# Branch and output GEMMs of two token mixers: fp32 matmuls replaced by three fp32r passes, with the low weight parts on GpSimd

## The chip, the core and the metric

The kernel runs on one core of a Trainium2 chip. The metric is device time in microseconds (us) of one execution; the kernel before took 2956.33 us (median of three runs, 2955.53 to 2958.14). The engines are named as in the profile: PE is TensorE's matmul, PEld its weight load, DVE is VectorE, ACT is ScalarE, POOL is GpSimd, and SP is SyncE, which here issues all the DMAs.

## The reference, cut to what matters

The program is a stack of two blocks of a conditioned transformer and then two blocks of a second model. The change touches only the end of `token_mixer`, which runs once in each of the first two blocks (`l` is 0 or 1; S is 256 tokens, the model width is 1024):

```python
def token_mixer(h, w_in, pool_w, pool_scale, rel_bias, lb, norm_g, w_branch, w_out):
    proj = h @ w_in
    ...
    y_a = pool_mixer(a, pool_w, pool_scale)            # 256 wide
    y_b = sparse_attention(q, k, v, qi, ki, wi, ...)   # 256 wide
    y_c = hgrn2(hq, hf, hi, hg, lb, norm_g)            # 512 wide
    g = jax.nn.sigmoid(gates.reshape(B, S, 3, D_MODEL))
    merged = (g[:, :, 0] * (y_a @ w_branch[:256])
              + g[:, :, 1] * (y_b @ w_branch[256:512])
              + g[:, :, 2] * (y_c @ w_branch[512:]))
    return merged @ w_out
```

All inputs and outputs are fp32.

## The kernel before, in words

Every engine has a hand-written program of its own, and semaphores order them. Activations lie feature by feature: 128 features on the partitions, 256 tokens along the free dimension. A weight matrix is read in panels of 1024 rows by 256 columns (1 MB), which SP loads into four slots in turn; slot n is loaded again when the panel four places earlier has been used (`load_static`). Four PSUM banks (`acc`) are used in turn as well.

Large GEMMs are already *split*: ACT copies each half panel (1024 x 128) into an fp32r tile, the high part (`high`), another engine subtracts it from the half panel, which gives the low part in place (`low`), and PE runs three fp32r matmuls: high weights by high data, high by low, low by high. In the first two blocks the low parts are made by DVE; in the second model's "even" and "up0" GEMMs by POOL. The gate, branch and output GEMMs of the mixers are plain: one fp32 matmul for each 128 x 128 weight tile and 256 tokens.

The end of the mixer, in the order of the program:

- `pool(l)`, `attention(l)` and `hgrn(l)` give `ymix`, eight groups of 128 features: groups 0 and 1 from the pool mixer, 2 and 3 from attention, 4 to 7 from hgrn. Between them stands `stage_end`, a barrier of PE, ACT and DVE. PE works on panels of the gate GEMM (`gate`) in between.
- `hgrn(l)` is a tree of eight levels (`lv` 0 to 7). At each level ACT takes two exponentials, DVE adds twice into running sums (`suff`, `pref`) and multiplies twice into `treeX` (all four of these DVE operations read two tiles in SBUF), and PE multiplies tiles of `treeX`. After level 7 PE forms the output (line 974), does gate panel 11, and spreads the norm (line 851).
- after a barrier comes the branch GEMM: 4 panels, each of 16 matmuls in three groups (`r` 0, 1, 2 for y_a, y_b, y_c), each group into its own bank. For each group DVE multiplies the bank by the gate (line 86, from PSUM) and, for `r` 1 and 2, adds the product to `merged` (line 86, two SBUF tiles).
- after another barrier comes the output GEMM `mixout` (4 panels of 16 matmuls, in `features`, line 674); DVE adds each panel to the residual (line 91), PE sums it for the layer norm.
- in between DVE carries the conditioning sums (`cond_weigh`, line 2115): scalar_tensor_tensor operations on 1024 elements that read a loaded panel and a row, both in SBUF. Layer 0 has one such step of two operations after each of the first three branch panels and one in front of each mixout residual; layer 1 has none at the branch, and a step of four operations at each mixout panel. SP loads their panels too, in one queue with the weights (`load_cond`), and waits there for the step before last (`cond_done`).

Of the kernel before, what the change touches and what calls it, by code (L numbers as in the profile page):

```python
# [20 lines left out]
P = 128  # L21
# [120 lines left out]
def plan():  # L142

    order = []
    for l in range(DEPTH):
        order += [Gemm(f"in{l}0", 22, split=True, kept=True), Gemm(f"out{l}0", 8, wide=True, panels_per_acc=2, split=True, kept=True),
                  Gemm(f"mix{l}", 15, split=True), Gemm(f"gate{l}", 12), Gemm(f"branch{l}", 4, 3), Gemm(f"mixout{l}", 4),
# [69 lines left out]
def program(nc, io):  # L217
    G, order, finished, _ = plan()
    w8, w11, wc = io["w8"], io["w11"], io["wc"]
    with ExitStack() as ctx:  # L220
# [120 lines left out]
        merged, mtmp = region(TMP, KD, T), region(TMP + 2048, 2, T)  # L341

# [154 lines left out]
        def split_parts(g, u, j):  # L497

            if g.name in kept_hi:
                hi = kept_hi[g.name][:, :, j * P:j * P + P]  # L500
            else:
                hi = (down_hi if g.wide else up_hi)[(2 * u + j) % 4]
            return hi, half_panel(g, u, j, slots_r)
# [5 lines left out]
        def wait_used(eng, g, it, u, j):  # L509
# [3 lines left out]
            elif g.ppa == 1:  # L513
                a = g.a0 + u
                eng.wait_ge(ready[a % BANKS], it + (a // BANKS + 1))
# [14 lines left out]
        def _(sp):  # L530
# [56 lines left out]
            for g in order:  # L587
# [35 lines left out]
                if g.name == "mix0":  # L623
                    sp.wait_ge(S("pair_ready"), 1)
                    for v, kept in enumerate((crow_d, crow2_d)):
                        sp.dma_start(kept.ap().rearrange("a (k t) -> a k t", k=4), pair_rows[v][0:1, :, :]).then_inc(S("row_stored"), 16)
                if g.name == "in00":
# [3 lines left out]
                    sp.wait_ge(S("bias_rows"), 1)  # L631
# [10 lines left out]
        def _(pe):  # L642
# [133 lines left out]
            def mix_tokens(g, u):  # L776
# [4 lines left out]
                for tb in range(2):  # L781
# [9 lines left out]
                    if tb == 1:  # L791
                        mm.then_inc(ready[b], 1)

# [213 lines left out]
            def ml_columns():  # L1007
# [6 lines left out]
                mm.then_inc(S("ml_cols"), 1)  # L1014
# [185 lines left out]
            def ssd_rates():  # L1200
                pe.wait_ge(S("dt_rows"), 1)
# [118 lines left out]
            for l in range(DEPTH):  # L1320
                for f in range(2):
                    if f == 1:
# [27 lines left out]
                        stage_end(pe, count)  # L1350
                        g = G[f"branch{l}"]
                        for u in range(4):
                            w = panel_in(g, 0, u)
                            for r, ks in enumerate((range(0, 2), range(2, 4), range(4, 8))):
                                b = acc_open(g, 0, u, r)
                                for j in range(2):
                                    for k in ks:
                                        mm = pe.matmul(acc[b][:, j * T:j * T + T], w[:, k * PANEL + j * P:k * PANEL + j * P + P],  # L1358
                                                       ymix[:, k, :], start=(k == ks[0]), stop=(k == ks[-1]))
                                mm.then_inc(ready[b], 1)  # L1360
                        stage_end(pe, count)
                        g = G[f"mixout{l}"]
                        for u in range(4):
                            features(g, 0, u, lambda k: merged[:, k, :], T)
# [6 lines left out]
                    def up_panel(it, u, name=f"in{l}{f}"):  # L1371
                        split_up(G[name], it, u, 2 * l + f)
                        if name == "in00" and isinstance(it, int) and (it, u) == (0, 3):
                            pe.wait_ge(S("loaded"), 64)
                            pe.matmul(mix[0:4, 0, 0:384], relb[:, :], const("onehot")[0:32, :], start=True, stop=True).then_inc(S("bias_mm"), 1)
# [1773 lines left out]
```

## Time and profile before

| what | value |
|---|---|
| median of the timed runs | 2956.33 us |
| span of the profiled execution | 2961.5 us (the profile holds this one execution, from its first to its last instruction) |
| PE busy | 2736.3 us (92%) |
| DVE busy | 1931.9 us (65%) |
| ACT busy | 1091.3 us (37%) |
| POOL busy | 183.3 us (6%) |
| mean granted PE clock | 0.977 |

An fp32 matmul of 128 x 256 leaves two records in the trace, an fp32r matmul one. A row of the timeline has its start and its duration in us (of a merged run of instructions, from the first start to the last end), then the engine, the line, the operation, output and inputs, the shape, the count, and in brackets the idle time before it and what ended it. `L476` in brackets is the barrier.

### The profile page before, as it was taken

The numbers are of one execution on the slowest core, as the hardware profiler recorded it, in microseconds if no ns is written. First come the engines' busy times: TensorE is split into PE (matmuls) and PEld (weight loads), VectorE is DVE, ScalarE is ACT, GpSimd is POOL, SyncE is SP. The second block draws the span as 40 slices with busy tenths as digits, with TensorE's granted clock in tenths as the row PEclk, the third lists the DMA queues.
The fourth block names the chain that finished last, engine by engine and source line by source line (L and its number), as shares of the span: only waits on it lengthen the run. The fifth ranks groups of instructions, "written<-read, shape, count | busy, mean of one in ns | idle before, by whom it ended". The sixth has DMA issues, their size and how long they took to land.

```text
span 2961.5 us, 48706 instructions
## 1 busy us (share of the span) xinstructions
PE 2736.3 (92%) x18394; PEld 2322.9 (78%) x18394; DVE 1931.9 (65%) x3303; ACT 1091.3 (37%) x1389; POOL 183.3 (6%) x85
## 2 busy tenths in 40 slices
PE   3999998999999988999988968999999899989998
PEld 3998977899999887799967854687744767668887
DVE  6776655677778666466746473577786676664781
ACT  2434432443543423154463542433300644442211
POOL 0000000000000000000012300244200000000000
PEclk9999999999999999999999989999999999999999
DMA  8775734677676553345512201122377221113442
GB/s 305 260 282 216 274 107 163 220 265 282 230 261 242 196 185 113 132 167 211 201 68 70 87 15 37 64 97 87 112 262 286 83 75 58 58 57 127 145 167 73
DMA packets 106383, 469.14 MB, mean 158 GB/s; under 512 B 7052, under 2 KB 57304, under 8 KB 58328
## 3 DMA queue, kind: packets, MB, share of 16 engines
q1 hardware_dynamic: 106200, 466.67, 43.7%
q8 instruction: 119, 1.95, 0.3%
q14 instruction: 64, 0.52, 0.1%
HBM read 465.58 MB, written 1.06 MB: 158 GB/s over the span
## 4 chain that ended last, share of the span: by engine, by line
PE 35%; DVE 10%; DVEq 7%; ACT 3%; issue 3%; ACTq 1%; DMA 1%; SPq 0%
PE accs L828 6%; DVEq L2830 4%; PE accs L689 4%; PE accs L674 4%; PE accs L690 4%; PE accs L691 4%; DVE arena L2807 3%; PE accs L1225 2%; PE accs L1227 2%; PE accs L1226 2%; DVE arena L2115 1%; PE accs L1358 1%; ACT arena L76 1%; PE mix L1282 1%; DVE arena L86 1%
## 5 line engine op out<-in xcount | busy, mean ns | idle before, releaser
L689 PE MATMUL accs<-normed_r,arena_r 128*128 128x256 f32 (+2 forms) x1864 | 585.0, 314 | 17.7 <-DVEq L2160 6.3
L691 PE MATMUL accs<-normed_r,panel_r 128*128 128x256 f32 (+2 forms) x1872 | 584.7, 312 | 0.0
L690 PE MATMUL accs<-arena_r 128*128 128x256 f32 x2069 | 584.5, 283 | 0.0
L86 DVE TENSOR_TENSOR panel_r<-panel,arena_r 128x1024 fp32r<-128x1024 f32 (+1 forms) x295 | 387.1, 1312 | 165.6 <-ACTq L1478 120.3
L1477 ACT ACTIVATE arena_r<-panel 128x1024 fp32r<-128x1024 f32 (+1 forms) x292 | 330.4, 1132 | 331.6 <-DMA panel<-w 145.3
L689 PEld LDWEIGHTS accs<-normed_r,arena_r 128*128 128x128 f32 (+1 forms) x1864 | 350.2, 188 | 55.4 <-issue 13.5
L690 PEld LDWEIGHTS accs<-arena_r 128*128 128x128 f32 x2069 | 389.5, 188 | 1.1 <-issue 0.2
L691 PEld LDWEIGHTS accs<-normed_r,panel_r 128*128 128x128 f32 (+1 forms) x1872 | 350.2, 187 | 23.8 <-issue 0.8
L674 PE MATMUL accs<-normed,panel 128*128 128x256 f32 x1536 | 344.5, 384 | 6.7 <-ACTq L476 3.0
L2807 DVE SCALAR_TENSOR_TENSOR arena<-accs,vectors,arena 128x189 f32<-128x189 f32 (+2 forms) x704 | 279.3, 428 | 95.4 <-issue 66.2
L674 PEld LDWEIGHTS accs<-normed,panel 128*128 128x128 f32 x1536 | 291.8, 192 | 54.1 <-issue 4.6
L1437 POOL TENSOR_TENSOR panel_r<-panel,arena_r 128x1024 fp32r<-128x1024 f32 x70 | 169.1, 2416 | 1953.7 <-ACTq L1485 1952.4
L828 PE MATMUL accs<-arena,panel 128*128 128x256 f32 (+1 forms) x832 | 256.3, 469 | 1.4 <-DVEq L2715 0.8
L828 PEld LDWEIGHTS accs<-arena,panel 128*128 128x128 f32 x832 | 157.9, 190 | 98.2 <-issue 85.8
L76 ACT ACTIVATE arena<-accs 128x512 f32<-128x512 f32 (+2 forms) x128 | 75.3, 589 | 372.4 <-PE accs L691 234.8
L689 PE MATMUL accs<-arena_r 128*128 128x256 f32 x704 | 200.1, 284 | 6.3 <-DVEq L2160 6.2
L691 PE MATMUL accs<-arena_r,panel_r 128*128 128x256 f32 x704 | 198.3, 282 | 0.0
L91 DVE SCALAR_TENSOR_TENSOR residual<-accs,mods,residual 128x256 f32<-128x256 f32 x96 | 46.4, 483 | 179.5 <-PE accs L828 86.8
L76 ACT ACTIVATE arena<-arena 128x512 f32<-128x512 f32 (+7 forms) x108 | 97.5, 903 | 162.6 <-DVEq L2753 58.6
L76 ACT ACTIVATE arena<-residual 128x512 f32<-128x512 f32 (+1 forms) x56 | 31.9, 569 | 328.6 <-DVEq L2860 279.1
L1484 ACT ACTIVATE arena_r<-panel 128x1024 fp32r<-128x1024 f32 x72 | 76.3, 1060 | 203.9 <-PE accs L691 188.1
L689 PEld LDWEIGHTS accs<-arena_r 128*128 128x128 f32 x704 | 133.2, 189 | 9.1 <-issue 5.3
(412 smaller groups left out, 4701.3 us busy)
## 6 DMA issues: line engine op xcount, KB each, us to landing
panel<-w SPq DMA_DIRECT2D x250, 1024.0 KB, 5.0
panel<-w SPq DMA_DIRECT2D x48, 1408.0 KB, 8.0
cond_panel<-wc SPq DMA_DIRECT2D x57, 1024.0 KB, 6.3
normed<-wc SPq DMA_DIRECT2D x43, 1024.0 KB, 6.8
arena<-wc SPq DMA_DIRECT2D x19, 1024.0 KB, 5.0
residual<-xs SPq DMA_DIRECT2D x2, 1024.0 KB, 9.7
residual<-wc SPq DMA_DIRECT2D x1, 1024.0 KB, 13.2
residual<-crows SPq DMA_DIRECT2D x2, 512.0 KB, 8.8
```

Source lines behind the costliest of these rows:

```text
L76: i = self.eng.activation(*a, **k)
L86: i = self.eng.tensor_tensor(*a, **k)
L674: mm = pe.matmul(acc[b][:, o:o + ntok], w[:, k * PANEL + j * P:k * PANEL + j * P + P], rhs(k), start=(k == 0), stop=(k == KD - 1))
L689: pe.matmul(out, hi[:, k, 0:m], src_hi(k), start=clear and k == 0, stop=False, skip_group_check=True)
L690: pe.matmul(out, hi[:, k, 0:m], src_lo(k), start=False, stop=False, skip_group_check=True)
L691: mm = pe.matmul(out, lo[:, k, 0:m], src_hi(k), start=False, stop=last and k == n - 1, skip_group_check=True)
L828: mm = pe.matmul(acc[a % BANKS][:, o:o + ntok], w[:, k * PANEL + j * P:k * PANEL + j * P + P], src(part * kper + k), start=first, stop=(pa ...
L1437: pool.tensor_tensor(lo, half_panel(g, u, j), hi, ALU.subtract)
L1477: act.eng.activation(split_parts(g, u, j)[0], half_panel(g, u, j), ACT.Copy)
L1484: act.eng.activation(split_parts(g, u, j)[0], half_panel(g, u, j), ACT.Copy)
L2807: dve.eng.scalar_tensor_tensor(out=out, in0=src, scalar=scale, in1=out, op0=ALU.mult, op1=ALU.add)
L2830: dve.drain()
```

## The change

Both GEMMs become split GEMMs of three fp32r passes. ACT makes all high parts: of `ymix`, of `merged`, and of the 16 half panels of each layer (in a ring of four tiles, `merge_ring`). POOL makes the low parts of `ymix` groups 0 to 3 and of all the half panels; DVE makes those of `ymix` groups 4 to 7 and of `merged`. The two barriers around the branch GEMM go; semaphores (`ymix_low`, `ymix_tail`, `merged_high`, `merged_low`, `low_made`) order the engines instead. The product that gives `ymix` groups 4 to 7 is done in two halves. To have enough semaphores, a number of one-shot ones elsewhere are merged into counting ones (`setup_act`, `decay_act`, `rates_dve` and so on); the order of work there is as before.

The core of the diff:

```diff
-... Gemm(f"branch{l}", 4, 3), Gemm(f"mixout{l}", 4),
+... Gemm(f"branch{l}", 4, 3, split=True), Gemm(f"mixout{l}", 4, split=True),
+        merged_hi, merged_lo = region(TMP + 2560, KD, T, of=arena_r), region(4096, KD, T, of=arena_r)
+        ymix_hi, ymix_lo = mix_hi, mix_lo
+        merge_ring = [region(off, KD, P, of=arena_r) for off in (0, 1024, 2048, TMP + 5888)]
...
 (PE)
+            def branch(l):
+                g = G[f"branch{l}"]
+                for u in range(4):
+                    for r, ks in enumerate((range(0, 2), range(2, 4), range(4, 8))):
+                        b = acc_open(g, 0, u, r)
+                        for j in range(2):
+                            if r == 0:
+                                pe.wait_ge(S("low_made"), split_count(g, 0, u, j))
+                            hi, lo = split_parts(g, u, j)
...
+                                pe.matmul(out, hi[:, k, :], ymix_hi[:, k, :], ...)
+                                pe.matmul(out, hi[:, k, :], ymix_lo[:, k, :], ...)
+                                mm = pe.matmul(out, lo[:, k, :], ymix_hi[:, k, :], ...)
+                            if r == 2 and j == 0:
+                                mm.then_inc(first_used, 1)
+                        mm.then_inc(ready[b], 1)
+            def mixed_out(l, u):
...
+                        if u == 0 and j == 0 and k % 2 == 0:
+                            pe.wait_ge(S("merged_low"), 4 * l + k // 2 + 1)
...
                         hgrn(l)
-                        stage_end(pe, count)
...
+                        branch(l)
-                        stage_end(pe, count)
 (POOL)
+            for l in range(DEPTH):
+                for n in range(2):
+                    pool.wait_ge(S("ymix_high"), 2 * l + n + 1)
+                    c = slice(2 * n, 2 * n + 2)
+                    pool.tensor_tensor(ymix_lo[:, c, :], ymix[:, c, :], ymix_hi[:, c, :], ALU.subtract)
+                    pool.drain().then_inc(S("ymix_low"), 1)
+                for name in ("branch", "mixout"):
+                    for u in range(4):
+                        low(G[f"{name}{l}"], 0, u)
 (ACT, at the end of pool, at the end of attention, in the levels of hgrn)
+                act.activation(ymix_hi[:, 0:2, :], ymix[:, 0:2, :], ACT.Copy).then_inc(S("ymix_high"), 1)
+                act.activation(ymix_hi[:, 2:4, :], ymix[:, 2:4, :], ACT.Copy).then_inc(S("ymix_high"), 1)
+                    if lv in (6, 7):
+                        high(G[f"branch{l}"], 0, lv - 6)
+            def branch(l):
+                for h in range(2):
+                    act.wait_ge(S("ymix_made"), 2 * l + h + 1)
+                    ... ymix_hi of two groups, then_inc(S("ymix_tail_high"), 1)
+                high(g, 0, 2)
+                high(g, 0, 3)
+                for u in range(4):
+                    act.wait_ge(S("merged"), 4 * l + u + 1)
+                    ... merged_hi of two groups, then_inc(S("merged_high"), 1)
+                    if u in (1, 2):
+                        for j in range(2):
+                            wait_used(act, g, 0, u + 1, j)
+                            high(out, 0, u - 1, (j,))
+                for u in range(2, 4):
+                    high(out, 0, u)
 (DVE)
+            def merged_low(l, u):
+                c = slice(2 * u, 2 * u + 2)
+                dve.wait_ge(S("merged_high"), 4 * l + u + 1)
+                dve.tensor_tensor(merged_lo[:, c, :], merged[:, c, :], merged_hi[:, c, :], ALU.subtract).then_inc(S("merged_low"), 1)
...
                     if u < CARRY.get(g.name, (0, 0))[1]:
                         cond_weigh(g.name, u, u % 2)
+                    if u >= 1:
+                        merged_low(l, u - 1)
+                merged_low(l, 3)
```

Where instructions move, three places matter.

POOL, from the start of the program (all its instructions up to the first loop). Before, after the constants, it has only the low parts of the second model's panels:

```order
L3141 MEMSET const-uint8-127 128x1
L1430 UNCONDITIONAL_BRANCH
L1437 ISA
L1437 TENSOR_TENSOR panel_r<-panel,arena_r 128x8x128 x26
L486 UNCONDITIONAL_BRANCH
```

And now; `decay_sums_r` is where `ymix_hi` and `ymix_lo` lie, and of the 16 low parts of a layer 8 belong to the branch GEMM and 8 to mixout:

```order
L1464 UNCONDITIONAL_BRANCH
L1478 ISA
L1478 TENSOR_TENSOR decay_sums_r<-arena,decay_sums_r 128x512 x2
L1471 TENSOR_TENSOR panel_r<-panel,arena_r 128x8x128 x16
L1478 TENSOR_TENSOR decay_sums_r<-arena,decay_sums_r 128x512 x2
L1471 TENSOR_TENSOR panel_r<-panel,arena_r 128x8x128 x42
```

Thirty-two subtractions of a half panel and four of `ymix` stand ahead of the 26 that were there.

ACT, the last levels of hgrn in layer 0 (the 8x64 and 4x128 rows are the exponentials of levels 6 and 7). Before:

```order
L76 ACTIVATE arena<-arena 128x16x32 x2
L76 ACTIVATE arena<-accs 128x512
L76 ACTIVATE arena<-arena 128x8x64 x2
L76 ACTIVATE arena<-arena 128x4x128 x2
L1663 ACTIVATE arena<-mix 32x8x32 x2
```

Now:

```order
L76 ACTIVATE arena<-arena 128x16x32 x2
L76 ACTIVATE arena<-accs 128x512
L76 ACTIVATE arena<-arena 128x8x64 x2
L1520 ACTIVATE arena_r<-panel 128x1024 x2
L76 ACTIVATE arena<-arena 128x4x128 x2
L1520 ACTIVATE arena_r<-panel 128x1024 x2
L1710 ACTIVATE arena<-mix 32x8x32 x2
```

The high parts of the first two branch panels stand behind the exponentials of these two levels.

DVE, the second branch panel of layer 0 (`arena<-accs,arena` is a product from PSUM, `arena<-arena` the add, the SCALAR_TENSOR_TENSOR pair is `cond_weigh`). Before:

```order
L86 TENSOR_TENSOR arena<-accs,arena 128x512 x2
L86 TENSOR_TENSOR arena<-arena 128x512
L86 TENSOR_TENSOR arena<-accs,arena 128x512
L86 TENSOR_TENSOR arena<-arena 128x512
L2115 SCALAR_TENSOR_TENSOR cond_panel,mods<-cond_panel,constants 128x1024 x2
```

Now:

```order
L86 TENSOR_TENSOR arena<-accs,arena 128x512 x2
L86 TENSOR_TENSOR arena<-arena 128x512
L86 TENSOR_TENSOR arena<-accs,arena 128x512
L86 TENSOR_TENSOR arena<-arena 128x512
L2181 SCALAR_TENSOR_TENSOR cond_panel,mods<-cond_panel,constants 128x1024 x2
L86 TENSOR_TENSOR arena_r<-arena,arena_r 128x512
```

The low part of `merged` of the panel before comes behind `cond_weigh`, so each panel has one DVE operation more.

## Rows read from the trace of the kernel before

**Rows 1.** The page, part 1: busy us, share of the span, instructions.

```profile
PE 2736.3 (92%) x18394; PEld 2322.9 (78%) x18394; DVE 1931.9 (65%) x3303; ACT 1091.3 (37%) x1389; POOL 183.3 (6%) x85
```

**Rows 2.** Groups by line and shape: count, busy us, mean ns; idle before.

```profile
L1358 PE MATMUL accs<-arena,panel 128*128 128x256 f32 x256 | 57.9, 390 | 2.8 <-ACTq L476 2.8
```

**Rows 3.** Stretch 600 to 620: us, PE, PEld, DVE, ACT, POOL busy (count), clock, DMA.

```profile
600.00:620.00 20.00, 19.78 (x166) 19.37 (x165) 15.68 (x19) 9.69 (x10) 0.00 (x0) 1.00 0.74 252
```

**Rows 4.** Timeline, layer 1: branch GEMM, mixout GEMM, last residual.

```profile
1212.69 27.89 PE L1358 MATMUL accs<-arena,panel 128*128 128x256 f32 x128 [1.40 <-ACTq L476]
...
1242.32 14.08 PE L674 MATMUL accs<-arena,panel 128*128 128x256 f32 x64 [1.74 <-DVEq L476]
...
1271.98 1.05 DVE L91 SCALAR_TENSOR_TENSOR residual<-accs,mods,residual 128x256 f32<-128x256 f32 x2 [1.79 <-PE accs L674]
```

**Rows 5.** Timeline, PE behind the barriers after pool and after attention, layer 0.

```profile
370.54 1.71 PE L903 MATMUL mix<-arena 64*128 64x128 f32 x16 [1.17 <-ACTq L476]
...
419.20 7.17 PE L674 MATMUL accs<-normed,panel 128*128 128x256 f32 x32 [0.75 <-ACTq L476]
```

**Rows 6.** Timeline, POOL's low parts beside DVE in the even GEMM.

```profile
1549.93 2.42 POOL L1437 TENSOR_TENSOR panel_r<-panel,arena_r 128x1024 fp32r<-128x1024 f32 x1 [0.18 <-issue]
1550.97 2.52 DVE L2439 SCALAR_TENSOR_TENSOR decay_sums<-panel,arena 128x512 f32<-128x512 f32 x2 [21.72 <-ACT arena L76]
...
1560.15 2.35 POOL L1437 TENSOR_TENSOR panel_r<-panel,arena_r 128x1024 fp32r<-128x1024 f32 x1 [7.81 <-ACTq L1485]
1560.80 2.25 DVE L2482 TENSOR_TENSOR arena<-arena 128x512 f32<-128x512 f32 x1 [0.17 <-issue]
1562.68 2.57 POOL L1437 TENSOR_TENSOR panel_r<-panel,arena_r 128x1024 fp32r<-128x1024 f32 x1 [0.18 <-issue]
1562.97 2.82 DVE L2483 TENSOR_TENSOR arena<-arena 128x512 f32<-128x512 f32 x1
```

**Rows 7.** Timeline, the same two engines, a DVE operation with an input in PSUM.

```profile
1643.81 2.41 POOL L1437 TENSOR_TENSOR panel_r<-panel,arena_r 128x1024 fp32r<-128x1024 f32 x1 [4.05 <-ACTq L1485]
1644.62 1.63 DVE L91 SCALAR_TENSOR_TENSOR arena<-accs,vectors,arena 128x510 f32<-128x510 f32 x2 [1.77 <-ACT arena L76]
```

**Rows 8.** Timeline, layer 0: levels 6 and 7 of hgrn, and what follows.

```profile
453.31 1.33 ACT L76 ACTIVATE arena<-arena 128x512 f32<-128x512 f32 x2 [0.98 <-DVEq L2396]
...
455.53 1.50 DVE L86 TENSOR_TENSOR arena<-arena 128x512 f32<-128x512 f32 x2
...
458.99 1.33 ACT L76 ACTIVATE arena<-arena 128x512 f32<-128x512 f32 x2 [4.35 <-PE mix L956]
460.35 1.46 DVE L86 TENSOR_TENSOR arena<-arena 128x512 f32<-128x512 f32 x2 [1.69 <-ACT arena L76]
...
463.96 0.79 PE L974 MATMUL mix<-arena 128*128 128x128 f32 x2 [0.87 <-DVEq L2377]
...
478.32 3.78 PE L851 MATMUL mix<-constants,rms_columns 128*128 128x128 f32 x16 [1.23 <-DVEq L2409]
```

**Rows 9.** Timeline, layer 0: branch and mixout, cond_weigh, SP's queue, ACT's high parts.

```profile
483.50 16.85 PE L1358 MATMUL accs<-arena,panel 128*128 128x256 f32 x67 [1.39 <-ACTq L476]
...
494.49 1.23 DVE L2115 SCALAR_TENSOR_TENSOR normed<-normed,constants 128x1024 f32<-128x1024 f32 x1
...
496.92 0.58 SPq L559 DMA_DIRECT2D normed<-wc  x1
...
497.54 1.13 SPq L536 DMA_DIRECT2D panel<-w  x2
...
515.50 14.08 PE L674 MATMUL accs<-arena,panel 128*128 128x256 f32 x64 [1.99 <-DVEq L476]
...
545.15 2.21 ACT L1477 ACTIVATE arena_r<-panel 128x1024 fp32r<-128x1024 f32 x2 [29.48 <-PE accs L674]
545.16 1.05 DVE L91 SCALAR_TENSOR_TENSOR residual<-accs,mods,residual 128x256 f32<-128x256 f32 x2 [4.24 <-PE accs L674]
```

**Rows 10.** DMA issues from 440 to 560: count, KB each, median us to landing.

```profile
panel<-w SPq DMA_DIRECT2D x12, 1024.0 KB, 7.4
```

More of the change, by code:

```diff
@@ L146, in plan @@
         order += [Gemm(f"in{l}0", 22, split=True, kept=True), Gemm(f"out{l}0", 8, wide=True, panels_per_acc=2, split=True, kept=True),
-                  Gemm(f"mix{l}", 15, split=True), Gemm(f"gate{l}", 12), Gemm(f"branch{l}", 4, 3), Gemm(f"mixout{l}", 4),
+                  Gemm(f"mix{l}", 15, split=True), Gemm(f"gate{l}", 12), Gemm(f"branch{l}", 4, 3, split=True), Gemm(f"mixout{l}", 4, split=True),
                   Gemm(f"in{l}1", 22, split=True, kept=True), Gemm(f"out{l}1", 8, wide=True, panels_per_acc=2, split=True, kept=True)]
@@ L500, in split_parts @@
                 hi = kept_hi[g.name][:, :, j * P:j * P + P]
+            elif g.name[:6] in ("branch", "mixout"):
+                hi = merge_ring[(2 * u + j) % 4]
             else:
@@ new lines, in mixed_out @@
+            def mixed_out(l, u):
+                g = G[f"mixout{l}"]
+                b = acc_open(g, 0, u)
+                for j in range(2):
+                    out = acc[b][:, j * T:j * T + T]
+                    pe.wait_ge(S("low_made"), split_count(g, 0, u, j))
+                    hi, lo = split_parts(g, u, j)
+                    for k in range(KD):
+                        if u == 0 and j == 0 and k % 2 == 0:
+                            pe.wait_ge(S("merged_low"), 4 * l + k // 2 + 1)
+                        pe.matmul(out, hi[:, k, :], merged_hi[:, k, :], start=(j == 0 and k == 0), stop=False, skip_group_check=True)
+                        pe.matmul(out, hi[:, k, :], merged_lo[:, k, :], start=False, stop=False, skip_group_check=True)
+                        mm = pe.matmul(out, lo[:, k, :], merged_hi[:, k, :], start=False, stop=(k == KD - 1), skip_group_check=True)
+                    mm.then_inc((first_used, ready[b])[j], 1)
@@ L1349, in _ @@
                         hgrn(l)
-                        stage_end(pe, count)
[L1351 to L1360, printed above, removed]
-                        stage_end(pe, count)
+                        branch(l)
                         g = G[f"mixout{l}"]
                         for u in range(4):
-                            features(g, 0, u, lambda k: merged[:, k, :], T)
+                            mixed_out(l, u)
                             if u >= 1:
@@ L1374, in up_panel @@
                             pe.wait_ge(S("loaded"), 64)
-                            pe.matmul(mix[0:4, 0, 0:384], relb[:, :], const("onehot")[0:32, :], start=True, stop=True).then_inc(S("bias_mm"), 1)
+                            pe.matmul(mix[0:4, 0, 0:384], relb[:, :], const("onehot")[0:32, :], start=True, stop=True).then_inc(S("setup_mm"), 1)
                     groups(pe, G[f"in{l}{f}"], up_panel, peel=True)
@@ L2426, in branch @@
                             dve.drain()
-                            dve.tensor_tensor(dst, dst, mtmp[:, :, :], ALU.add)
+                            i = dve.tensor_tensor(dst, dst, mtmp[:, :, :], ALU.add)
+                            if r == 2:
+                                i.then_inc(S("merged"), 1)
                         dve.drain()
```

100 lines of the change are left out of this document (59 added, 41 removed).

## The prediction

> **What bounds the kernel now.** I read the page's shares first: PE is busy 92% of the span, DVE 65%, POOL 6% [rows 1]. So PE time saved near the end of the mixer is time saved, unless PE comes to wait. Then PE's own prices. The grouped view shows the branch GEMM as 256 records, two for each fp32 matmul [rows 2]. For an fp32r matmul of that shape I take a stretch full of them: 166 in 20 us at full clock, 0.12 us each [rows 3], so three passes cost 0.36. In the timeline of layer 1 the branch GEMM is 128 records, 64 fp32 matmuls, in 27.89 us, 0.436 each [rows 4]. A panel of 16 tiles goes from 6.97 to 48 x 0.12 = 5.8 us, 1.2 less. Sixteen panels give 19 us, and that is all PE can win.
>
> Around these GEMMs PE waits little now: 1.4 us before branch and 1.7 before mixout in layer 1 [rows 4], 1.2 and 0.75 behind the barriers after pool and attention, both released by ACT [rows 5]. The question is what the new work on the other engines does to that.
>
> **The price of a low part on POOL.** The even GEMM shows these two engines side by side. POOL takes 2.41 us for a half panel. A DVE operation with two SBUF inputs that falls beside one takes 2.25 or 2.82 us [rows 6], where the same shape alone takes 0.73 (two in 1.46 in hgrn, [rows 8]); it ends some 0.5 us after POOL does. Two scalar_tensor_tensor operations took 2.52 together. A DVE operation with an input in PSUM is not touched: two in 1.63 with POOL beside them [rows 7]. So the two exclude each other. The order matters too: POOL's next low part began at 1562.68, before DVE's next add at 1562.97, and that add waited for all of it [rows 6]. POOL and DVE then alternate, one low part for each DVE operation, and a DVE operation that finds POOL just begun waits about 2.15 us (2.82 less 0.73 is 2.1; the schedule gives 2.0 to 2.2).
>
> The Trainium skill, page "SBUF — State Buffer", section "SBUF: two separate sides", says that DVE and GpSimd share a port pair which is an exclusive lock, held by whichever starts first for its whole instruction, and that a DVE operation with two SBUF inputs takes it against a GpSimd operation that reads SBUF. By that rule `cond_weigh` is blocked as well, and the sum is the one below; the trace agrees for the adds (2.82 in place of 0.73) and no row shows it for an accumulating operation.
>
> **The change part by part**, layer 0 / layer 1, in us against the trace of before. I worked it out as a hand schedule: each engine's instructions in the order of the changed program, with durations from rows, and POOL and DVE excluding each other as above. B is the start of the branch matmuls.
>
> 1. Copies of `ymix` after pool and attention. Each stands on ACT ahead of a barrier where PE waits for ACT [rows 5]. An ACT operation of 512 columns takes 0.66 [rows 8]. Two of them: **+1.3 / +1.3**. POOL's low parts there are hidden (POOL is empty and the next reader is the branch GEMM).
>
> 2. Levels 6 and 7 of hgrn. ACT makes the high halves of two branch panels behind the exponentials, so four POOL low parts meet six DVE operations with two SBUF inputs, four of level 6 and two of level 7 [rows 8]. PE, ACT and DVE wait for each other there in a ring, so a wait of DVE is the path. Four collisions: 2.0 + 3 x 2.15 = 8.5; of it 1.7 falls in the idle time before level 7's pair, and a blocked operation finishes about 0.1 sooner. Line 974 comes **+6.4 / +6.4** later. Without exclusion 1.8 would stay, because ACT's two high halves of 1.1 us [rows 9] stand ahead of the copy which PE needs for line 974.
>
> 3. The barrier before the branch GEMM. Now `r` 0 and 1 need only groups 0 to 3, and the high and low parts of 4 to 7 are ready just as `r` 1 ends. The 1.4 us [rows 4] go: **-1.4 / -1.4**. The spread of 3.78 us [rows 8] stays in front.
>
> 4. From B to the start of mixout, 32.0 us before in layer 0 (515.50 - 483.50, [rows 9]) and 29.6 in layer 1 [rows 4]. Layer 0: SP's queue is in order, and branch panel 3 stands behind a `cond_weigh` load which waits until DVE's first step is done: 496.92, B + 13.4 [rows 9]. That point stays, so the two loads land at about B + 21.9 (7.4 us from issue, [rows 10]). ACT, in order, makes panel 3's two high halves (2.2) and only then the first copy of `merged`. DVE, which has that low part next, has been idle since B + 19.8 and goes on at B + 24.8. It still has 14 tensor_tensor operations at 0.82 with the gap and one `cond_weigh` step of two at 1.23 [rows 9]: 13.9. Behind the waiting DVE everything is queued: the gate products that free the banks, the step that lets SP load, the low parts for mixout. Six of its operations meet low parts of POOL (branch panel 3, mixout panels 0 and 1): 0.6 + 0.5 + 1.3 + 2.2 + 2.4 + 2.2 = 9.2, of which 0.8 falls into idle time. The last low part of `merged` is made at B + 47.1; three of the four pieces of mixout's first half panel (18 matmuls, 2.1 us) are done by then, so mixout counts as started at B + 45.0. That is 13.0 more; 1.0 is added because PE, which has waited, may open at half clock, as the 67 records in 16.85 us show that it now does (78 would fit at 0.218 each, [rows 9]): **+14**. Layer 1 has no `cond_weigh` here, its loads come early, and the waits sum to 10.0, mostly in time that DVE had idle: start at B + 30.2, **+0.6**. (Free of exclusion: 35.0 and 24.3.)
>
> 5. From there to the last residual, 29.7 before in both layers (545.16 - 515.50, 1271.98 - 1242.32). Layer 0: PE sets it, 4 x 5.8 and the same 1.7 of other work: 24.9, **-4.8**. Layer 1: DVE has 16 `cond_weigh` operations (19.7) and four residuals at 1.05 [rows 4], 24.2 with gaps, of which the last residual lies behind the point; it starts them 2.1 after mixout's counted start, and POOL's low parts cost 7.7 of waits: 2.1 + 23.1 + 7.7 = 32.9, **+3.2**. Here a second engine becomes the bound. Free of exclusion PE would set it with 25.8, -3.9.
>
> Layer 0: 1.3 + 6.4 - 1.4 + 14 - 4.8 = +15.5. Layer 1: 1.3 + 6.4 - 1.4 + 0.6 + 3.2 = +10.1. Together **+25.6** on the profiled 2961.5, 2987.1; the median of the runs is 5.2 below that span, so I forecast **2982**.
>
> The two least certain prices. No row has `cond_weigh` beside a low part. The nearest below is the PSUM pair that is free [rows 7], by which the sum is +12.6 (layer 1's mixout then is PE's again); the nearest above is the scalar_tensor_tensor pair from two SBUF tiles [rows 6], by which it is +25.6. I take the latter, since `cond_weigh` reads two SBUF tiles. The other is the length of a low part and the moment at which loads land: with 2.2 to 2.6 us and landings 2 us to either side, the schedule gives +21 to +31. The semaphores merged elsewhere I cost at nothing: the order of work there is the same, and an increment takes the place of an increment.
>
> **The rivals.**
>
> A. DVE and POOL don't exclude each other in these places. Then layer 0 is 1.3 + 1.8 - 1.4 + 3.0 - 4.8 = -0.1 and layer 1 is 1.3 + 1.8 - 1.4 - 5.3 - 3.9 = -7.5: 2948.7, faster. It decides at the point where a DVE add beside a low part stays at 0.73. Rows 7 speak for it, rows 6 against, with the very shapes of hgrn's adds.
>
> B. They do, but DVE gets in between low parts about every second time, or ACT spaces the high halves so that POOL pauses. Half the collisions give about +9: 2965. Against it: DVE asked second at 1562.97 and lost [rows 6].
>
> C. The longer waits (6 us before line 974, several at branch panel 3 and in front of mixout) put PE at half clock afterwards, which costs 2 us more at two or three places (layer 0's branch GEMM now lost 2.4 by it, 16.85 - 67 x 0.218, [rows 9]): +4 to +6, 2987.
>
> The three passes may also take up to 0.40, where they are cut into short runs between waits; PE sets the time in layer 0's mixout alone (64 tiles), so that is 64 x 0.04 = 2.6 us, and it lies in the range.
>
> **How the numbers follow.** Forecast 62%, C 10%, B 16%, A 12%. A change of 0.2% (5.9 us) is about what can be told from none. A is faster with 0.11, the rest of it and a sliver of B no change, 0.07; slower 0.82. The forecast's own range is 2976 to 2992 (+21 to +31 on the span, and the tiles' price). Down to B's lower half at 2958 and up to C's end at 2994 it leaves out A and little else.
>
> **What would show it.** In the trace after: adds on `arena` in levels 6 and 7 of 2 to 2.9 us, each ending half a us after one of POOL's low parts (if they stay at 0.73, A). Line 974 some 6 us later behind gate panel 10's end. SP's load of branch panel 3 still behind `cond_weigh`, DVE idle about 5 us ahead of the first low part of `merged`. PE's waits in mixout's first half panel released by DVE. In layer 1 the residuals, not PE, late in each mixout panel, and `cond_weigh` pairs of 4 us where POOL works. Wrong would be: POOL's low parts much shorter than 2.4, `cond_weigh` at 1.23 beside them, or a first barrier after pool that costs nothing more.

## The result and the profile after

The changed kernel takes 2989.43 us (median of four runs, 2986.14 to 2991.66) against 2955.93 for the kernel before: a ratio of 1.0111, 95% interval 1.0099 to 1.0123. It is slower by 33.5 us; forecast were 2982 us and a range of 2958 to 2994.

The page of after, part 1 (busy us, share of the span, instructions), beside [rows 1]:

```profile
PE 2728.8 (91%) x18650; PEld 2328.6 (78%) x18650; DVE 1987.8 (67%) x3317; ACT 1135.2 (38%) x1437; POOL 272.6 (9%) x121
```

PE has lost 7.5 us of busy time where 19 were to be had, and DVE has gained 56, although few operations were added (14 records, some 9 us by their lengths when alone): the others last longer. The timeline of layer 0 shows which; here levels 6 and 7 of hgrn and what follows (columns as in [rows 8], which answers to it; `L1471` is the low part on POOL):

```profile
455.14 3.45 DVE L86 TENSOR_TENSOR arena<-arena 128x512 f32<-128x512 f32 x2
455.49 2.56 POOL L1471 TENSOR_TENSOR panel_r<-panel,arena_r 128x1024 fp32r<-128x1024 f32 x1 [35.25 <-ACTq L1521]
...
457.80 0.70 PE L1001 MATMUL mix<-arena 128*32 128x32 f32 x32
...
458.23 2.58 POOL L1471 TENSOR_TENSOR panel_r<-panel,arena_r 128x1024 fp32r<-128x1024 f32 x1 [0.18 <-issue]
...
458.76 5.41 DVE L86 TENSOR_TENSOR arena<-arena 128x512 f32<-128x512 f32 x2 [0.17 <-issue]
...
461.28 2.35 POOL L1471 TENSOR_TENSOR panel_r<-panel,arena_r 128x1024 fp32r<-128x1024 f32 x1 [0.47 <-ACTq L1521]
...
463.81 2.58 POOL L1471 TENSOR_TENSOR panel_r<-panel,arena_r 128x1024 fp32r<-128x1024 f32 x1 [0.18 <-issue]
...
464.34 3.36 DVE L86 TENSOR_TENSOR arena<-arena 128x512 f32<-128x512 f32 x2 [0.17 <-issue]
...
470.77 0.80 PE L1019 MATMUL mix<-arena 128*128 128x128 f32 x2 [0.86 <-DVEq L2443]
```

Three pairs that took 1.50, 1.46 and 1.46 us now take 3.45, 5.41 and 3.36, 7.8 more together, around the four low parts. Line 974 of before is line 1019 here; the PE row of 128x32 is the last level matmul ahead of it. The branch and the mixout GEMM of layer 0, from several engines ([rows 9] answers; the branch GEMM starts at B = 489.27):

```profile
498.55 3.20 DVE L2181 SCALAR_TENSOR_TENSOR normed<-normed,constants 128x1024 f32<-128x1024 f32 x1
...
502.96 0.58 SPq L564 DMA_DIRECT2D normed<-wc  x1
503.58 1.13 SPq L541 DMA_DIRECT2D panel<-w  x2
...
512.00 2.21 ACT L1520 ACTIVATE arena_r<-panel 128x1024 fp32r<-128x1024 f32 x2 [15.28 <-DMA panel<-w]
...
514.97 1.08 DVE L86 TENSOR_TENSOR arena_r<-arena,arena_r 128x512 fp32r<-128x512 f32 x1 [5.43 <-ACT arena_r L76]
...
515.70 0.55 PE L816 MATMUL accs<-decay_sums_r,arena_r 128*128 128x256 f32 x1 [7.39 <-POOLq L1472]
...
521.78 3.19 DVE L2181 SCALAR_TENSOR_TENSOR normed<-normed,constants 128x1024 f32<-128x1024 f32 x1
...
533.48 1.47 DVE L86 TENSOR_TENSOR arena_r<-arena,arena_r 128x512 fp32r<-128x512 f32 x2
...
559.12 1.05 DVE L91 SCALAR_TENSOR_TENSOR residual<-accs,mods,residual 128x256 f32<-128x256 f32 x2 [2.63 <-PE accs L836]
```

The `cond_weigh` operations of 1.23 us now take up to 3.2 here. SP's panel 3 goes out behind the cond panel at 502.96, ACT gets it at 512.00, DVE has waited 5.43 us by 514.97 and PE 7.39 by 515.70. The last low part of `merged` ends at 534.95, B + 45.7. In layer 1's mixout DVE is the bound; its timeline beside POOL ([rows 4] answers with its last residual):

```profile
1278.14 3.17 POOL L1471 TENSOR_TENSOR panel_r<-panel,arena_r 128x1024 fp32r<-128x1024 f32 x1 [6.24 <-ACTq L1521]
1281.49 3.15 POOL L1471 TENSOR_TENSOR panel_r<-panel,arena_r 128x1024 fp32r<-128x1024 f32 x1 [0.18 <-issue]
...
1279.02 3.38 DVE L2181 SCALAR_TENSOR_TENSOR cond_panel<-cond_panel,residual 128x1024 f32<-128x1024 f32 x1
...
1282.48 3.25 DVE L2181 SCALAR_TENSOR_TENSOR constants<-cond_panel,residual 128x1024 f32<-128x1024 f32 x1
...
1287.01 1.06 DVE L91 SCALAR_TENSOR_TENSOR residual<-accs,mods,residual 128x256 f32<-128x256 f32 x2
...
1293.13 1.05 DVE L91 SCALAR_TENSOR_TENSOR residual<-accs,mods,residual 128x256 f32<-128x256 f32 x2
```

The two wait for each other: POOL's low part, 2.4 alone, takes 3.17 beside a running `cond_weigh`, and the next `cond_weigh` waits for POOL. No residual there shows idle time in front of it.

### The profile page after: what moved, and what is told of

It reads as the page before. It is cut to its first block, busy times and chain, and to the rows that moved or that the text cites. A ratio compares the mean times of both kernels' runs of the same rounds, so it can differ in the third digit from the quotient of the medians.

```text
span 2984.4 us, 49420 instructions
## 1 busy us (share of the span) xinstructions
PE 2728.8 (91%) x18650; PEld 2328.6 (78%) x18650; DVE 1987.8 (67%) x3317; ACT 1135.2 (38%) x1437; POOL 272.6 (9%) x121
## 4 chain that ended last, share of the span: by engine, by line
PE 51%; DVE 24%; DVEq 9%; ACT 6%; issue 5%; DMA 3%; ACTq 1%; SPq 1%
PE accs L694 8%; PE accs L695 7%; PE accs L696 7%; PE accs L873 6%; PE accs L679 6%; DVEq L2913 4%; DVE panel_r L86 4%; DVE arena L86 3%; DVE arena L2890 3%; DMA panel<-w 2%; ACT arena L76 2%; PE accs L1270 2%; PE accs L1271 2%; PE accs L1272 2%; DVE constants L2181 1%
## 5 line engine op out<-in xcount | busy, mean ns | idle before, releaser
L1520 ACT ACTIVATE arena_r<-panel 128x1024 fp32r<-128x1024 f32 (+1 forms) x324 | 364.3, 1124 | 342.7 <-DMA panel<-w 172.1
L695 PEld LDWEIGHTS accs<-arena_r 128*128 128x128 f32 x2069 | 390.0, 189 | 1.2 <-issue 0.2
L1471 POOL TENSOR_TENSOR panel_r<-panel,arena_r 128x1024 fp32r<-128x1024 f32 x102 | 253.3, 2483 | 864.8 <-ACTq L1528 692.2
L86 DVE TENSOR_TENSOR arena<-arena 128x512 f32<-128x512 f32 (+8 forms) x151 | 139.6, 925 | 35.1 <-ACT arena L76 16.0
```

What stands on the lines that cost most here:

```text
L86: i = self.eng.tensor_tensor(*a, **k)
L695: pe.matmul(out, hi[:, k, 0:m], src_lo(k), start=False, stop=False, skip_group_check=True)
L1471: pool.tensor_tensor(lo, half_panel(g, u, j), hi, ALU.subtract)
L1520: act.eng.activation(split_parts(g, u, j)[0], half_panel(g, u, j), ACT.Copy)
```

## The experiments

All are compared by their timed medians and by four points of their traces: PE's start behind the barrier ahead of the pool mixer, its first level matmul of hgrn (`128x32`), B, and the last residual.

### The kernel before, on the same chip

> The kernel before, unchanged, for a profile of the same chip as the runs beside it. The profiles of before and after differ by 22.9 us of span, the timed medians by 33.5. My theory accounts for +25.8 us at the ends of the two mixers (16.5 in layer 0, 9.3 in layer 1, read from the two traces) and for nothing elsewhere. If the profile of before was only one of the longer executions, this profile has a span near 2954 us, and the difference of 7 lies in stretches that the change doesn't touch (granted clock). If the rest of the program really slows down with the change (a rival: PE's clock after its new waits), then the stretches behind the two mixers are shorter here than in the profile of after by about 7 us, always in the same place.

Measured: 2959.09 us (2955.13 to 2961.45) beside 2955.65 for the other runs of the same kernel, ratio 1.0009 (0.9998 to 1.0019); its profile has a span of 2957.1. The points, in us:

| point | layer 0: e1 | after | layer 1: e1 | after |
|---|---|---|---|---|
| barrier ahead of pool | 351.80 | 351.85 | 1081.46 | 1095.39 |
| first level matmul of hgrn | 424.66 | 426.13 | 1153.32 | 1168.66 |
| B | 481.50 | 489.27 | 1210.64 | 1230.24 |
| last residual | 543.10 | 559.12 | 1269.93 | 1293.13 |

From the barrier to the last residual layer 0 has 191.30 and 207.27 (+16.0), layer 1 188.47 and 197.74 (+9.3): 25.2 us in the two mixers. The spans differ by 27.3. The rest lies in code whose order the change leaves as it was: between the two layers after is 2.1 faster (543.10 to 1081.46 against 559.12 to 1095.39), behind layer 1 it is 4.1 slower (1687.2 against 1691.3). That last stretch is 1685.3 to 1691.4 us long in all the profiles here (1687.3 in e2, 1691.4 in e6, 1688.0 in e4). So the profile of before in [rows 1] was one of the longer executions, as the theory had it. The expected 2954 was not reached: e1's profiled execution took 2959.11 us itself, 3.5 above the median of the runs beside it.

### Low parts that take POOL a fifth of the time

```diff
-                    pool.tensor_tensor(lo, half_panel(g, u, j), hi, ALU.subtract)
+                    pool.tensor_tensor(lo[:, 0:n, :], half_panel(g, u, j)[:, 0:n, :], hi[:, 0:n, :], ALU.subtract)
...
 (PE, branch and mixout)
-                                mm = pe.matmul(out, lo[:, k, :], ...)
+                                mm = pe.matmul(out, lo[:, 0, :], ...)
```

Here n is 1 for branch and mixout.

> As the kernel after, but POOL subtracts only the first 128 of the 1024 columns of each half panel in branch and mixout, and PE reads that one low tile in all eight places (the low parts of the others are left out; all instructions of PE, ACT, DVE and SP stay, with their order and waits). Theory (POOL's low parts and DVE's operations with two SBUF inputs exclude each other): POOL's 36 pieces take about 0.4 us, the waits of DVE go, and my schedule gives 34 us less than after (16 in layer 0, 18 in layer 1): 2955, within 0.2% of before or a little under it. Rival (the loss is due to ACT's added copies, the in-order queues and PE's waits, not to the exclusion): only the latency of a low part goes, 2 us where PE waits for one, some 5 to 10 us in all: 2980 or more.

Measured: 2957.95 us (ratio to before 1.0004, 0.9992 to 1.0015), 31.5 less than after, where 34 were expected. A low part alone takes POOL 0.46; one row of POOL and one of DVE, layer 0:

```profile
494.12 0.46 POOL L1471 TENSOR_TENSOR panel_r<-panel,arena_r 128x128 fp32r<-128x128 f32 x1 [28.10 <-ACTq L1521]
...
510.85 0.69 DVE L86 TENSOR_TENSOR arena_r<-arena,arena_r 128x512 fp32r<-128x512 f32 x1 [5.80 <-ACT arena_r L76]
```

All of ACT's copies, the in-order queues and the added DVE operations are still there, so they aren't the 31.5 us; POOL's long subtractions are. What it also shows: without them the split brings nothing either. DVE still stands idle in layer 0 ahead of the first low part of `merged`, 5.80 us.

### POOL busy, but only writing

e2 with two more instructions behind each short subtraction:

```diff
+                    if n < KD:
+                        for _ in range(2):
+                            pool.drain()
+                            pool.memset(half_panel(g, u, j)[:, n:KD, :], 0.0)
```

> As e2_short_lows, but POOL, after each short subtraction, sets the other 896 columns of the half panel to zero, twice, so that it is busy again for each half panel but reads nothing in SBUF for most of that time (the low parts of seven of eight tiles are left out, as in e2). Theory by rows so far (a POOL operation that reads two SBUF tiles excludes DVE's operations with two SBUF inputs): DVE's operations beside the writing POOL keep 0.69 and 1.22 us, and the time is that of e2 plus the longer wait for a low part, 2960 to 2966. Rival (any POOL operation on SBUF excludes them): DVE's operations stretch to the length of POOL's writes, and the time is close to after, 2975 to 2990.

Measured: 2954.72 us (0.9993, 0.9983 to 1.0004). The timeline of layer 0, DVE and POOL side by side:

```profile
508.56 1.81 POOL L1475 MEMSET panel<- 128x896 f32 x2
510.90 1.40 POOL L1471 TENSOR_TENSOR panel_r<-panel,arena_r 128x128 fp32r<-128x128 f32 x1 [0.53 <-issue]
...
508.78 0.69 DVE L86 TENSOR_TENSOR arena<-arena 128x512 f32<-128x512 f32 x1
509.61 1.23 DVE L2185 SCALAR_TENSOR_TENSOR normed<-normed,constants 128x1024 f32<-128x1024 f32 x1
...
510.76 1.22 DVE L2185 SCALAR_TENSOR_TENSOR normed<-normed,constants 128x1024 f32<-128x1024 f32 x1
```

POOL is busy from 508.56 to 510.37 and DVE's operations beside it keep 0.69 and 1.23. (From one subtraction to the next, 505.42 to 507.98, POOL needs 2.56 us, as in after: 513.15 to 515.69.) The short subtraction behind, which reads, takes 1.40 in place of 0.46: now POOL is the one that waits, until DVE's operation of 510.76 is done. Over both mixers, the time that DVE's 128x512 tensor_tensor operations from two SBUF tiles have above 0.69, and `cond_weigh` above 1.22, sums to 1.6 us here, 45.9 in after and 0.4 in e1. From here on these are called DVE's waits. So it isn't POOL being busy, nor the latency of a low part (2.4 us here too), but two engines that read. The Trainium skill, page "SBUF — State Buffer", section "SBUF: two separate sides", limits the lock of a DVE operation with two SBUF inputs to a GpSimd operation that reads SBUF; this run agrees, and so do the accumulating `cond_weigh` operations of after (3.20 in place of 1.23), for which no row of before spoke.

### Branch panel 3 ahead of the cond panel

```diff
-                        load_static(g, i)
+                        if (g.name, i) != ("branch0", 3):
+                            load_static(g, i)
+                        if (g.name, i) == ("branch0", 2):
+                            load_static(g, 3)
```

> As the kernel after, but in layer 0 SP loads branch panel 3 ahead of the third cond_weigh panel, so that it doesn't wait for DVE's first cond_weigh step. Theory (term 4: panel 3 lands at B + 22.7, ACT makes its high halves ahead of the first copy of merged, and DVE stands idle for 5.4 us): DVE's idle time there goes and layer 0 ends 5.2 us earlier, 2984 us; layer 1 stays. Rival (DVE is bound there anyway by POOL's low parts, which would then only fall closer together): 0 to 2 us less, 2987 to 2989.

Measured: 2986.24 us (2981.92 to 2988.88), 3.2 below after, whose runs (2986.14 to 2991.66) overlap with these; the trace has to decide. In it layer 0 takes 68.7 us from B to the last residual, where after takes 69.85: 1.1 less, not 5.2. DVE, in layer 0:

```profile
498.72 3.20 DVE L2184 SCALAR_TENSOR_TENSOR normed<-normed,constants 128x1024 f32<-128x1024 f32 x1
...
501.85 3.38 DVE L2184 SCALAR_TENSOR_TENSOR normed<-normed,constants 128x1024 f32<-128x1024 f32 x1
...
512.64 0.69 DVE L86 TENSOR_TENSOR arena_r<-arena,arena_r 128x512 fp32r<-128x512 f32 x1 [0.47 <-issue]
...
518.94 3.15 DVE L2184 SCALAR_TENSOR_TENSOR normed<-normed,constants 128x1024 f32<-128x1024 f32 x1
...
522.03 3.35 DVE L2184 SCALAR_TENSOR_TENSOR normed<-normed,constants 128x1024 f32<-128x1024 f32 x1
```

The idle time is gone (0.47 for 5.43), but panel 3's low parts now run earlier and meet `cond_weigh`: four operations of 3.2 to 3.4 us where after has two. DVE's waits in layer 0 rise from 22.0 to 27.6 us, about what the idle time had been. The last low part of `merged` ends at B + 44.1 in place of 45.7. The mechanism that I had named is there and worth 1 to 2 us; the rival was nearer.

### The same load order, with low parts that hardly exclude

e6 and the edit of e3 together.

> e6_write_only_pool (low parts that hardly exclude DVE, seven of eight low tiles left out) with the edit of e3_panel3_first. In e3 DVE's idle time ahead of the first low part of merged went, but the last residual of layer 0 came only 0.8 us earlier, because the low parts of panel 3 then met both cond_weigh steps. Theory (the loss at the branch has two causes in a row, SP's queue and the exclusion, and each hides the other): without the exclusion the same edit gives 4 to 5 us in layer 0, 2950 us. Rival (panel 3's landing was never on the path): no more than 1 us here as well, 2954 or more. It is also the bound for this split: what it would bring with low parts that cost DVE nothing.

Measured: 2951.47 us (0.9979, 0.9968 to 0.9989); e6 was 2954.72 beside its own runs of before (0.9993, 0.9983 to 1.0004). The two intervals still touch, so what follows rests on the traces. The last low part of `merged` ends at B + 32.1 here and at B + 36.9 in e6: 4.8 us, as expected. The last residual comes 56.4 after B, against 59.5, 3.1 earlier. The rest goes, as far as the rows show, at mixout's opening, where PE has waited and runs at half clock (granted clock 0.50, the lower of its two levels); in e6, where PE's last wait in mixout's first half panel ends at 517.97, the same two stretches have 0.89 and 1.00. The stretches 512 to 518 and 518 to 524 of e9 (us, busy time of PE, PEld, DVE, ACT and POOL, clock, DMA):

```profile
512.00:518.00 6.00, 3.41 (x16) 3.41 (x17) 5.30 (x8) 1.01 (x2) 3.38 (x5) 0.50 0.68 263
518.00:524.00 6.00, 6.00 (x50) 6.00 (x50) 2.98 (x7) 1.74 (x2) 3.95 (x5) 0.95 0.79 299
```

From B to the last residual layer 0 takes 69.85 us in after, 68.7 with the queue's cause removed (e3), 59.5 with the exclusion's (e6), 56.4 with both. So the queue and the exclusion are two causes behind each other: removing the first alone lets the second take its place. 2951.47 against 2957.25 is also about what the change could bring with low parts that cost DVE nothing and the better load order: 6 us.

### The first four low parts by DVE

```diff
 (POOL)
-                    for u in range(4):
+                    for u in range(2 if name == "branch" else 0, 4):
 (DVE, hgrn)
                 take(8)
+                for u in range(2):
+                    low(G[f"branch{l}"], 0, u)
```

> As the kernel after, but the low parts of branch panels 0 and 1 are made by DVE, after its last copy of hgrn's levels, where it waits for PE; ACT's high parts stay where they are. Theory (four collisions in levels 6 and 7 put line 974 off by 6.4 us, of which 1.8 comes from ACT's high parts): line 974 comes 4.6 us earlier in each layer, 9.3 us in all, 2980 us. Rival (ACT's four high halves are what delays hgrn): 0 to 2 us a layer less, 2985 or more.

Measured: 2982.23 us, 7.2 less than after (expected 9.3). PE in layer 0:

```profile
460.79 0.70 PE L1001 MATMUL mix<-arena 128*32 128x32 f32 x32
...
469.17 0.79 PE L1019 MATMUL mix<-arena 128*128 128x128 f32 x2 [0.87 <-DVEq L2443]
```

Line 1019 follows the last level matmul of 32 columns after 8.4 and 8.3 us in the two layers; in after it was 13.0, in e1 5.8 and 6.1. That is the 4.6 of the theory, twice, and 2.2 to 2.6 stay for ACT's high halves (expected 1.8). Layer 0 gives most back: from B to the last residual it takes 73.7 us for 69.85, since another `cond_weigh` operation meets a low part:

```profile
520.47 3.20 DVE L2181 SCALAR_TENSOR_TENSOR normed<-normed,constants 128x1024 f32<-128x1024 f32 x1
...
523.59 3.37 DVE L2181 SCALAR_TENSOR_TENSOR normed<-normed,constants 128x1024 f32<-128x1024 f32 x1
```

In after the second of the pair took 1.22. From the first level matmul to the last residual the traces keep 1.6 and 2.1 us of the two 4.6; the medians differ by more (runs of 2973.23 to 2984.63). An earlier start moves low parts and DVE operations against each other, and the number that meet changes.

### Low parts in four pieces

```diff
-                    pool.tensor_tensor(lo, half_panel(g, u, j), hi, ALU.subtract)
+                    step = 2 if g.name[:6] in ("branch", "mixout") else KD
+                    for k in range(0, KD, step):
+                        pool.tensor_tensor(lo[:, k:k + step, :], half_panel(g, u, j)[:, k:k + step, :], hi[:, k:k + step, :], ALU.subtract)
```

> As the kernel after, but POOL makes each low part of branch and mixout in four subtractions of 256 columns. Theory (what one holds is held for one instruction, so a DVE operation waits for the piece that runs and no more): a piece takes about 0.75 us by the 0.46 of 128 columns in e2 and the 2.4 of 1024, a DVE operation beside one waits 0.6 us and no longer 2.1; a low part takes 3.5 us. DVE's waits fall from about 46 us in all to 15 to 25, and the time by some 15 us to 2975. Rival (DVE gets in only when POOL has no more work queued): a DVE operation waits for all four pieces, 3 us, and the time is 2990 to 3000.

Measured: 2977.33 us (1.0068, 1.005 to 1.0085), 12 below after. DVE's waits in the mixers sum to 17.9 us (45.9 in after), inside the expected 15 to 25: what excludes is held for one instruction. It runs the other way as well; the timeline of levels 6 and 7, and one row of layer 1's mixout:

```profile
457.48 2.10 DVE L86 TENSOR_TENSOR arena<-arena 128x512 f32<-128x512 f32 x2 [0.17 <-issue]
...
455.82 4.34 POOL L1473 TENSOR_TENSOR panel_r<-panel,arena_r 128x256 fp32r<-128x256 f32 x4 [35.72 <-ACTq L1523]
...
464.26 2.77 POOL L1473 TENSOR_TENSOR panel_r<-panel,arena_r 128x256 fp32r<-128x256 f32 x4 [0.18 <-issue]
...
1260.68 6.65 POOL L1473 TENSOR_TENSOR panel_r<-panel,arena_r 128x256 fp32r<-128x256 f32 x4 [0.18 <-issue]
```

Four pieces take POOL 2.77 us alone and 4.34 beside DVE. In layer 1's mixout (the last row) they take up to 6.65, and POOL works there without a pause: from B to the last residual it is 66.8 us, in after 62.9. From the first level matmul to the last residual layer 0 gains 6.0 us and layer 1 nothing.

### Eight pieces, with the edits of e3 and e4

`step = 1` in the edit of e7, and the two diffs above.

> The kernel after with all its work, with three edits: POOL's low parts in eight pieces of 128 columns, branch panel 3 loaded ahead of the third cond_weigh panel (as in e3), and the low parts of branch panels 0 and 1 by DVE (as in e4). Theory (the exclusion is held for one instruction, and 0.46 us for 128 columns is the least that a DVE operation waits): DVE's waits of 46 us shrink to about a quarter, though a low part takes 5 us and PE waits for it; 2960 to 2968, still above before. Rival (smaller pieces only collide more often, since POOL is busy twice as long): about as e7_pieces, 2974 to 2980.

Measured: 2987.83 us (1.0105, 1.0087 to 1.0123), as slow as after: both the theory's time and the rival's were wrong. DVE's waits did shrink, to 7.2 us. But POOL, in layer 0's mixout:

```profile
531.78 3.37 POOL L1476 TENSOR_TENSOR panel_r<-panel,arena_r 128x128 fp32r<-128x128 f32 x8 [0.18 <-issue]
535.33 5.40 POOL L1476 TENSOR_TENSOR panel_r<-panel,arena_r 128x128 fp32r<-128x128 f32 x8 [0.18 <-issue]
540.90 3.38 POOL L1476 TENSOR_TENSOR panel_r<-panel,arena_r 128x128 fp32r<-128x128 f32 x8 [0.18 <-issue]
544.46 5.32 POOL L1476 TENSOR_TENSOR panel_r<-panel,arena_r 128x128 fp32r<-128x128 f32 x8 [0.18 <-issue]
```

It works without a pause at 3.4 to 5.4 us a half panel, 9 us a panel, where PE needs 5.8, and PE waits for it. The wait has moved from DVE to POOL, and POOL is the bound.

### The semaphores alone

Branch and mixout stay plain fp32 GEMMs; the high and low parts, with their semaphores, are left out of after.

```diff
 (PE, branch)
+                                if u == 0 and j == 0 and r == 2 and k % 2 == 0:
+                                    pe.wait_ge(S("ymix_made"), 2 * l + k // 2 - 1)
...
 (PE, mixout)
+                        if u == 0 and j == 0 and k % 2 == 0:
+                            pe.wait_ge(S("merged"), 4 * l + k // 2 + 1)
```

> One part of the change alone: branch and mixout stay plain fp32 GEMMs, with no high or low parts, and the two barriers are replaced by semaphores (PE waits for ymix groups 4 to 7 in two halves at r = 2 of the first branch panel, and for each pair of merged groups in mixout's first half panel). Theory (the barriers cost PE's idle time that stands behind them, 1.4 us before branch, 1.7 to 2 before mixout and part of what lies between): branch starts 2 us earlier (no barrier behind the spread), mixout about 2 us earlier, in each layer: 8 us less than before, 2948. Rival (the waits behind the barriers are those for the data themselves, for DVE's product at the branch and its last add at mixout): only the barrier's own latency goes, 0.5 us in each place, 2 us in all, 2953 to 2956, the same as before.

Measured: 2949.87 us beside 2955.58 for before, ratio 0.998 (0.997 to 0.9989): 6 us faster (expected 8). PE in layer 0; [rows 9] has the two rows of before with 1.39 and 1.99 of idle time in front:

```profile
479.87 28.39 PE L810 MATMUL accs<-arena,panel 128*128 128x256 f32 x128
508.10 13.98 PE L823 MATMUL accs<-arena,panel 128*128 128x256 f32 x64
```

No idle time stands in front of either GEMM; PE works through from the spread to the last panel. From B to the last residual it is 57.8 us in both layers (61.6 and 59.3 in e1). This is the version to keep: 0.987 of after's time, with PE at its plain fp32 price. Beside it e9 shows what the split itself does: from B to the last residual e9 is 1.4 and 6.5 us shorter in the two layers, but from the barrier ahead of pool to B 5.5 and 4.7 longer, where ACT's copies and high parts stand. No run takes those away alone.

### The kernel after again

> The kernel after, unchanged, on the chip of the runs beside it: 2984 to 2990 us, 28 to 34 above before, with the sums of the two mixer ends that the first profile of it has (+16 in layer 0, +9 in layer 1). If the time is nearer to 2982, what the median of the first runs had above my sum is scatter between executions.

Measured: 2989.17 us beside 2955.58 (1.0108, 1.009 to 1.0126), and a span of 2986.9. From the barrier to the last residual it has 208.06 and 200.67 us, 16.8 and 12.2 more than e1 (+16.0 and +9.3 in the first profile); from B, 71.1 and 63.3 (69.85 and 62.9). The 33 us are no scatter of the first four runs.

## Why the prediction was right, point by point

The sign, the mechanism and most terms held; the time came out 7.4 us above the forecast, inside the range.

| step | forecast, layer 0 / 1 | measured, after less e1 (the two rows without a sign: after) |
|---|---|---|
| 1: barrier to first level matmul | +1.3 / +1.3 | +1.4 / +1.4 |
| 2: line 974 later | +6.4 / +6.4 | +7.2 / +6.9 |
| 2 and 3: first level matmul to B | +5.0 / +5.0 | +6.3 / +4.3 |
| 4: last low part of `merged` behind B | 47.1 / 32.3 | 45.7 / 32.2 |
| 5: from there to the last residual | 23.8 / 30.8 | 24.2 / 30.7 |
| 4 and 5: B to the last residual | +9.2 / +3.8 | +8.3 / +3.6 |
| together | +15.5 / +10.1 | +16.0 / +9.3 |

Step 2 takes line 974 (1019) from the last level matmul of 32 columns, 5.8 and 6.1 us in e1. The sum for the two mixers, +25.6, measures 25.2, and 29.0 in e8.

Two things were off. The first is the sum against the medians. These differ by 33.5, the spans of the profiles by 27.3 (after) and 29.8 (e8), the two mixers by 25.2 in after and 29.0 in e8. I had taken the untouched code as equal and subtracted 5.2 for a profile of before above its median. The profiled executions are no median ones either: e1's took 2959.11 where before has 2955.93, after's 2986.14 where after has 2989.43, 6.5 us together. So 4.5 to 8 us of the medians' difference are in no stretch that I can point to. Which stretches are longer or shorter in a median execution stays open: behind layer 1 both profiles of after have 1691.3 where e1 has 1687.2, but e6 and e9 have 1691.4 and aren't slower than before, and e4, with most of the change, has 1688.0.

The second is inside step 4. Its sum came near (45.7 for 47.1) by two errors that partly cancel: DVE's idle time ended at B + 25.7, 0.9 later than forecast, and the six operations behind it that meet low parts lost 6.2 us and not 8.4. And its causes are not a sum. I had put its 13 us down to SP's queue, DVE's idle time behind it and the collisions one after the other, and so expected 5.2 from freeing the queue. e3 gave 1.1 there. e9 explains it: without the exclusion the same edit brings the end of `merged` 4.8 us forward. The two are not added; whichever is left fills the time.

Rival A, no exclusion, was priced at -7.6 us: e6, where it hardly exists, has 0.9 us less than before in the medians and, from the barrier to the last residual in its two layers, 189.56 and 183.56 us, 6.6 less than e1. So the sum of its price came near in the traces, though not its layers (-1.7 and -4.9 for -0.1 and -7.5), and what made it wrong was its condition, as [rows 6] had said. Rival B, half the collisions, fell: 7.8 us of waits in each hgrn, all three pairs hit, as [rows 6] with its alternating order had it. Rival C is partly in: after's last branch panel and mixout's opening in layer 0 run at half clock, two stretches (columns as above):

```profile
512.00:518.00 6.00, 1.62 (x6) 1.35 (x6) 2.65 (x4) 5.42 (x6) 4.67 (x2) 0.50 0.96 396
...
530.00:536.00 6.00, 1.78 (x8) 1.78 (x9) 5.13 (x8) 0.63 (x1) 1.15 (x1) 0.59 0.61 236
```

In the first PE has just waited 7.39 us; there DVE is late anyway, so it costs little. Ahead of B it even differed between layers. Beside e1, line 1019 to gate panel 11 is 1.0 us longer in layer 0 and 1.2 shorter in layer 1 (granted clock 0.50 from 470 to 476 us, 0.74 from 1214 to 1220), the spread takes 3.38 us in layer 0 and 2.05 in layer 1, and the levels ahead of the last are 1.7 longer in layer 1. So steps 2 and 3 came to 6.3 in one and 4.3 in the other. By the time alone C, with its 2987, was nearer to 2989.43 than the forecast of 2982. In the first profile the mixers' 25.2 leave no room for its 4 to 6 us beside the other terms; the 29.0 of e8 leave about 3.

The range also held 2.6 us for three passes of up to 0.40 us, which the rows do not bear out: where PE ran without a wait (490 to 500 in after) it made 86 matmuls in 10.00 us, 0.35 for three.

## What to carry to other kernels

Before work is moved from DVE to an idle POOL, look in the trace for an operation with two SBUF inputs on DVE beside a reading one on POOL and compare its length with the same shape alone: here one low part, 2.4 us of POOL's time, cost a DVE operation up to 2.2 us, so an engine at 6% was not free. Two causes of one wait are not added; take both away in turn and together before one is blamed. And test the small part of a change by itself: the semaphores alone were worth 6 us (e5), and semaphores and three passes together, with low parts that cost DVE almost nothing, no more (e9).

## What the runs showed of the hardware

- The exclusion between POOL and DVE is for one instruction at a time and in both directions. Low parts in one piece of 1024 columns cost DVE 45.9 us in the two mixers (after), in four pieces 17.9 (e7), in eight 7.2 (e10); POOL's own time for a half panel went from 2.4 (up to 3.5 beside `cond_weigh`) to 2.8 to 6.7 and 3.4 to 8.7.
- POOL writes of 896 columns (0.9 us each, e6) left DVE's operations at 0.69 and 1.23, so reading on POOL's side is what matters.
- A subtraction of 128 columns takes POOL 0.46 us (e2), of 1024 columns 2.4 (after). By a straight line through the two, an estimate, about 0.18 of it is there for any size.
